# Second block's input products: ten pairs of output tiles by seven block products, and rope keys split in the Fourier phase

## What is computed

```python
# second block
proj = h @ w_in[i]
(s5_u, fq, fk, fv, ff, rw, sq, sk, sv, gates) = _split(proj, IN_SPLIT_SIZES)
y_s5 = _s5_mixer(s5_u, ...)      # bu = einsum(ug, bb); associative_scan; y = einsum(x, c) + d * ug; gelu, glu
...
# first block, in each of its two layers
k_rope = apply_rope(k_r, cos[None], sin[None])
k = concatenate([k_nope, broadcast_to(k_rope, ...)], axis=-1)
```

## Time and profile before

| | us |
|---|---|
| median of three runs | 3330.05 (3327.62 to 3330.68) |
| the profiled execution | 3330.66 |
| its span | 3328.9 |
| PE busy | 3184.9 (96% of the span) |
| DVE busy | 2051.6 (62%) |
| ACT busy | 1010.0 (30%) |
| POOL busy | 937.2 (28%) |

### The profile page before, as it was taken

One profiled execution on the slowest core, in us unless ns is written; L12 is line 12 of the kernel. 1 busy time (PEld: TensorE's weight loads), 2 busy tenths in 40 slices (PEclk: granted clock), 3 DMA queues, 4 the chain that ended last, 5 costly groups with the idle time before them and its releaser, 6 DMA issues. The chain is left out here.

```text
span 3328.9 us, 41783 instructions
## 1 busy us (share of the span) xinstructions
PE 3184.9 (96%) x17082; PEld 2716.1 (82%) x17082; DVE 2051.6 (62%) x2422; ACT 1010.0 (30%) x1456; POOL 937.2 (28%) x617
## 2 busy tenths in 40 slices
PE   8998999999899999999999999999999999999997
PEld 7997888999688898888868986766777787888875
DVE  5535664444476544547466545555676666897788
ACT  2113432101233320000122222555433543444644
POOL 3320001333000033333224322000241453555575
PEclk9999999999999999999999999999999999999998
DMA  3120000211100013323330004111461454455453
GB/s 137 45 65 9 21 1 20 78 45 45 33 29 1 7 45 144 125 104 97 108 129 33 1 29 121 36 45 36 137 221 67 140 166 152 142 178 174 146 158 120
DMA packets 111758, 282.12 MB, mean 85 GB/s; under 512 B 15010, under 2 KB 20770, under 8 KB 111552
## 3 DMA queue, kind: packets, MB, share of 16 engines
q1 hardware_dynamic: 107104, 263.19, 24.2%
q10 hardware_dynamic: 4464, 16.25, 1.2%
HBM read 237.37 MB, written 41.42 MB: 84 GB/s over the span
## 5 line engine op out<-in xcount | busy, mean ns | idle before, releaser
L3672 PE MATMUL psum<-x,w_hi 128*128 128x512 f32 x2016 | 627.0, 392 | 8.3 <-DVE x L3643 3.2
L199 POOL CAST w_hi<-w_raw 128x1024 fp32r<-128x1024 f32 x116 | 125.7, 1083 | 1765.6 <-PE psum L212 1092.5
L3672 PEld LDWEIGHTS psum<-x,w_hi 128*128 128x128 f32 x2016 | 379.0, 189 | 93.5 <-issue 7.0
L3672 PE MATMUL psum<-x,w_lo 128*128 128x512 f32 x1008 | 393.4, 390 | 0.0
L3557 POOL TENSOR_TENSOR w_lo<-w_sum,w_hi 128x512 fp32r<-128x512 f32 x180 | 251.1, 1402 | 333.0 <-ACT w_hi L3551 333.0
L745 PE MATMUL psum<-h,w_hi 128*128 128x512 f32 x1024 | 327.6, 401 | 11.1 <-PEq L126 7.4
L203 POOL TENSOR_TENSOR w_lo<-w_raw,w_hi 128x1024 fp32r<-128x1024 f32 x116 | 302.1, 2605 | 16.4 <-DVE y L1554 7.2
L745 PEld LDWEIGHTS psum<-h,w_hi 128*128 128x128 f32 x1024 | 189.9, 191 | 58.7 <-issue 17.4
L3672 PEld LDWEIGHTS psum<-x,w_lo 128*128 128x128 f32 x1008 | 189.9, 188 | 39.7
L212 PE MATMUL psum<-hn_hi,w_hi 128*128 128x348 f32 x864 | 188.7, 327 | 16.4 <-DVE hn_lo L409 14.9
L745 PE MATMUL psum<-h,w_lo 128*128 128x512 f32 x512 | 202.5, 395 | 0.0
(11 more groups left out here) (464 smaller groups left out, 6468.2 us busy)
## 6 DMA issues: line engine op xcount, KB each, us to landing
w_raw<-in_w_mlp SPq DMA_DIRECT2D x169, 256.0 KB, 2.9
norm_factor<-in_w_mlp SPq DMA_DIRECT2D x87, 256.0 KB, 2.9
w_raw<-in_w_mlp SPq DMA_DIRECT2D x42, 512.0 KB, 3.4
w_raw<-in_w_in SPq DMA_DIRECT2D x36, 512.0 KB, 3.4
w_raw<-in_w_gates SPq DMA_DIRECT2D x32, 512.0 KB, 4.0
gates_kept<-gate_stage SPq DMA_DIRECT2D x64, 256.0 KB, 2.2
gates<-gates_kept SPq DMA_DIRECT2D x32, 512.0 KB, 3.3
w_raw<-in_w_out SPq DMA_DIRECT2D x24, 512.0 KB, 3.5
```

The costliest lines, as they stand in the source:

```text
L199: self.core.nc.gpsimd.tensor_copy(self.hi[:, g % 2], self.raw[:, g % 2]).then_inc(self.hi_done, 1)
L3672: last = self.core.nc.tensor.matmul(out, one[:, k, :], other[:, k, :], start=(group == 0 and k == 0 and part == 0), stop=(group == second ...
```

## The change

The 23 tiles are made in another order and another way. Three tiles stay plain: the two of S5 and the forget gates. The other twenty form ten pairs of neighbours. A pair is a product of a weight of 2x2 blocks (two output tiles by two halves of K) with a right side of 2x2 blocks (two halves of K by two halves of the tokens); it is made by the Strassen-Winograd scheme in seven block products of 4 k-blocks x 3 passes = 12 matmuls of 128x512 (tensor_pair). Each product has its own PSUM bank, eight in turn.

The right-hand sums are made once and kept in SBUF (vector_sums): for kk = 0 to 3 four sums of 128x512, their high parts on ACT (scalar_sums) and their low parts on DVE, from rows of h that ACT has first multiplied in place by the norm weight (scalar_rows). For each pair DVE makes four weight sums (vector_weights, and vector_last_weight for the block S4), ACT the seven high parts, POOL the seven low parts, in a ring of four half-tiles. ACT copies the first product out; DVE adds the others up in four quarters and scales each by r (vector_first, vector_second: seven adds, four scalings), and SP stores each quarter. The rows of h now need only r (one operation of 1024 columns in the first eight pairs).

The S5 parameters move with it: angle after pair 2, coefficients after pair 4, powers after pair 5, shift powers after 6 and 7, fin in the middle of the last pair, and hout goes to the S5 phase (vector_outs), where DVE makes it after all stores have landed. u and ug lie where the sums lay, so SP loads them in the S5 phase too, after the last store and the last product. PE there transposes with ident, no longer with masks, and waits for the rows only after the transposes, and for hout before the Toeplitz row.

In the first block kr_hi and kr_lo are made at the end of the rope step in the Fourier phase; the head tensors are placed below the Fourier ones for that.

```diff
...
+class PairedProducts:
+    A11, A12, S2, S1, S3, S4, A22 = range(7)
+    BANKS = (2, 5, 3, 4, 0, 1, 6, 7)
+    U, X, V, W = range(4)
+    STEPS = 11
+    FREED_BY = (0, 1, 2, 6, 5, 8, 10)
...
+    def store(self, sp, p, i, step):
+        m = PAIRS2[p][0 if i in (self.X, self.V) else 1]
+        cols = slice(0, CH2) if i in (self.X, self.U) else slice(CH2, T2)
+        sp.wait_ge(self.step, self.STEPS * p + step)
+        sp.dma_start(self.io["proj2"][m][:, cols], self.quarter(p, i)).then_inc(self.stored[(4 * p + i) % 6], 16)
...
+    def scalar_rows(self, act, x_lo):
+        for n in range(KT):
+            k = n // 2 + n % 2 * (KT // 2)
+            act.wait_ge(x_lo, k + 1)
+            self.core.nc.scalar.activation(self.rows(k), self.rows(k), ACT.Copy, scale=self.scale(k)) \
+                .then_inc(self.scaled, 1)
...
+    def scalar_weight(self, act, x):
+        p, j = divmod(x, 7)
+        if j in (self.S1, self.S3, self.S2, self.S4):
+            act.wait_ge(self.w_sums, 4 * p + (self.S1, self.S3, self.S2, self.S4).index(j) + 1)
+        else:
+            self.loaded(act, p)
+        if self.before[x] is not None:
+            act.wait_ge(self.done, self.before[x] + 1)
+        self.core.nc.scalar.activation(self.ring(self.w.hi, x), self.source(x), ACT.Copy).then_inc(self.w_hi_done, 1)
...
+    def pool_weight(self, pool, x):
+        pool.wait_ge(self.w_hi_done, x + 1)
+        self.core.nc.gpsimd.tensor_tensor(self.ring(self.w.lo, x), self.source(x),
+                                          self.ring(self.w.hi, x).bitcast(F32), ALU.subtract) \
+            .then_inc(self.w_lo_done, 1)
...
+    def tensor_pair(self, pe, p):
+        nc = self.core.nc
+        for j in range(7):
+            x = 7 * p + j
+            pe.wait_ge(self.w_lo_done, x + 1)
+            if x >= 8:
+                q, freed = divmod(x - 8, 7)
+                if freed == self.A11:
+                    pe.wait_ge(self.copied, q + 1)
+                else:
+                    pe.wait_ge(self.step, self.STEPS * q + self.FREED_BY[freed])
+            dst = self.core.psum[:, self.bank(p, j), :]
+            w_hi, w_lo = self.ring(self.w.hi, x), self.ring(self.w.lo, x)
+            for kk in range(KT // 2):
+                b_hi, b_lo = self.moving(j, kk)
+                if p == 0 and j in (self.S1, self.S3, self.S2, self.A22):
+                    pe.wait_ge(self.t_lo_done, 4 * kk + (self.S1, self.S3, self.S2, self.A22).index(j) + 1)
+                for part, (one, other) in enumerate(((w_hi, b_hi), (w_hi, b_lo), (w_lo, b_hi))):
+                    last = nc.tensor.matmul(dst, one[:, kk, :], other, start=(kk == 0 and part == 0),
+                                            stop=(kk == KT // 2 - 1 and part == 2))
+            last.then_inc(self.done, 1)
...
+    def vector_sums(self, dve, kk):
+        nc, raw = self.core.nc, self.t_raw
+        first, second = slice(0, CH2), slice(CH2, T2)
+        upper, lower = self.rows(kk), self.rows(KT // 2 + kk)
+        dve.wait_ge(self.scaled, 2 * kk + 2)
+        nc.vector.tensor_tensor(raw[:, 0, kk, :], upper[:, second], upper[:, first], ALU.subtract).then_inc(self.t_sums, 1)
+        nc.vector.tensor_tensor(raw[:, 1, kk, :], lower[:, second], upper[:, second], ALU.subtract) \
+            .then_inc(self.t_sums, 1)
+        dve.wait_ge(self.t_sums, 4 * kk + 1)
...
+    def vector_last_weight(self, dve, p):
+        raw, half = self.raw(p), KT // 2
+        dve.wait_ge(self.w_lo_done, 7 * p + self.A12 + 1)
+        dve.wait_ge(self.w_sums, 4 * p + 3)
+        self.core.nc.vector.tensor_tensor(raw[:, 0, half:], raw[:, 0, half:], self.temps[:, 1], ALU.subtract) \
+            .then_inc(self.w_sums, 1)
...
+    def vector_first(self, dve, p):
+        before = self.STEPS * p
+        dve.wait_ge(self.copied, p + 1)
+        self.quarter_free(dve, p, self.X)
+        self.vector_add(dve, p, self.A12, self.X, self.U)
+        self.vector_last_weight(dve, p)
+        self.vector_add(dve, p, self.S2, self.U, self.U)
+        dve.wait_ge(self.step, before + 1)
+        self.vector_scale(dve, p, self.X)
+        dve.wait_ge(self.step, before + 2)
+        self.quarter_free(dve, p, self.V)
+        self.vector_add(dve, p, self.S1, self.V, self.U)
...
+            for p in range(pairs.n):
+                pairs.store(sp, p, pairs.X, 3)
+                sp.wait_ge(pairs.w_lo_done, 7 * (p + 1))
+                if p + 2 < pairs.n:
+                    pairs.load(sp, p + 2)
+                if p == pairs.n - 1:
+                    w.load(sp, g0 + plain)
+                    w.load(sp, g0 + plain + 1)
+                if p < KT:
+                    sp.wait_ge(h_normed, p + 1)
+                    sp.dma_start(io["h_kept"][p], row(p)).then_inc(h_stored, 16)
+                pairs.store(sp, p, pairs.W, 7)
+                pairs.store(sp, p, pairs.V, 9)
+                pairs.store(sp, p, pairs.U, 11)
...
+            for p in range(pairs.n):
+                if p == 0:
+                    x.wait_read_out(pe, plain - 2)
+                    x.wait_read_out(pe, plain - 1)
+                pairs.tensor_pair(pe, p)
...
+            pairs.scalar_rows(act, x.x_lo)
+            store(0)
+            pairs.scalar_sums(act, 0)
+            pairs.scalar_sums(act, 1)
+            store(1)
+            act.wait_ge(w.tile_done, g0 + 2)
+            pairs.scalar_weight(act, 0)
+            pairs.scalar_weight(act, 1)
+            pairs.scalar_sums(act, 2)
+            pairs.scalar_sums(act, 3)
+            act.wait_ge(w.tile_done, g0 + 3)
+            pairs.scalar_weight(act, 2)
+            pairs.scalar_weight(act, 3)
+            store(2)
...
+            tile(0)
+            pairs.vector_sums(dve, 0)
+            pairs.vector_sums(dve, 1)
+            tile(1)
+            pairs.vector_weights(dve, 0)
+            pairs.vector_sums(dve, 2)
+            pairs.vector_sums(dve, 3)
+            tile(2)
+            for p in range(pairs.n):
+                pairs.vector_first(dve, p)
+                if p + 1 < pairs.n:
+                    pairs.vector_weights(dve, p + 1)
                 else:
-                    x.vector_tile(dve, m, stage[:, m % 2, :], ATT_SCALE if query else 1.0)
-                if m < KT:
-                    nc.vector.scalar_tensor_tensor(out=h_all[:, m, :], in0=h_all[:, m, :], scalar=vecs[:, m:m + 1],
-                                                   in1=r, op0=ALU.mult, op1=ALU.mult).then_inc(h_normed, 1)
-                if m == KT + 1:
+                    dve.wait_ge(pairs.w_lo_done, 7 * p + pairs.S1 + 1)
+                    s5.vector_in(dve, 0)
+                    s5.vector_in(dve, 1)
...
+                pairs.vector_second(dve, p)
+                if p < KT:
+                    nc.vector.tensor_tensor(row(p), row(p), r[:, META:META + T2], ALU.mult).then_inc(h_normed, 1)
+                if p == 2:
                     s5.vector_angle(dve)
-                if m == KT + 3:
+                if p == 4:
                     s5.vector_coefficients(dve)
-                if m == KT + 4:
+                if p == 5:
                     s5.vector_powers(dve)
-                if m == KT + 5:
-                    s5.vector_shift_powers(dve)
-                if m in (KT + 6, KT + 7):
-                    s5.vector_out(dve, 0, SC, m - KT - 6)
-                if m in (KT + 8, KT + 9):
-                    s5.vector_out(dve, SC, SC + 1, m - KT - 8)
-                if m in (KT + 10, KT + 11):
-                    s5.vector_in(dve, m - KT - 10)
-    return BranchesEnded(core.weights, x.g0 + N_PROJ2, stored, h_stored)
+                if p in (6, 7):
+                    s5.vector_shift_powers(dve, range(1, 4) if p == 6 else range(4, 7))
...
+            act.wait_ge(kr_ready, 1)
+            for half in range(2):
+                nc.scalar.activation(kr_hi[64 * half:64 * half + 64], slots[0:64, KR, :], ACT.Copy) \
+                    .then_inc(kr_hi_done, 1)
...
+            nc.vector.tensor_tensor(kr, kr, krs, ALU.add).then_inc(kr_ready, 1)
+            dve.wait_ge(kr_ready, 1)
+            dve.wait_ge(kr_hi_done, 2)
+            nc.vector.tensor_tensor(kr_lo[0:64], kr, kr_hi[0:64].bitcast(F32), ALU.subtract)
+            nc.vector.tensor_tensor(kr_lo[64:P], kr_hi[64:P].bitcast(F32), kr_hi[64:P].bitcast(F32), ALU.subtract)
...
-            for half in range(2):
-                nc.scalar.activation(kr_hi[64 * half:64 * half + 64], kr, ACT.Copy).then_inc(kr_hi_done, 1)
...
-            dve.wait_ge(kr_hi_done, 2)
-            nc.vector.tensor_tensor(kr_lo[0:64], kr, kr_hi[0:64].bitcast(F32), ALU.subtract).then_inc(kr_lo_done, 1)
-            nc.vector.tensor_tensor(kr_lo[64:P], kr_hi[64:P].bitcast(F32), kr_hi[64:P].bitcast(F32), ALU.subtract) \
-                .then_inc(kr_lo_done, 1)
...
+    def vector_outs(self, dve):
+        self.link(self.core.nc.vector.memset(self.hout[:], 0.0))
+        for n0, n1 in ((0, SC), (SC, SC + 1)):
+            for part in range(2):
```

(10 more changed lines are left out.)

337 lines of the change are left out of this document (243 added, 94 removed).

## The result

The changed kernel takes **3339.73 us** (median of six runs, 3333.36 to 3347.93) against 3330.36 for the kernel before (six runs): a ratio of 1.0028, with a 95% interval of 1.0016 to 1.0040. It is slower by 9 us. The forecast was 3325.0 with a range up to 3338, so the result lies 1.7 us above the range and on the side that had the smallest chance.

A forecast was written before the change was run, and what follows sets the result against it. PE was taken to bound the input products of the second block. The terms -27.2 + 15.1 + 1.6 + 3 + 12.7 - 10.4 gave -5.2 us against the median of 3330.05, so 3325.0 us, range 3312 to 3338 (8 in 10).

The forecast's parts named there:

- (a): Input products of the second block: 840 matmuls instead of 960, 120 fewer at 0.227 us each, -27.2 us.
- (b): Start of the changed stage: PE waits for DVE's work before the first pair, +15.1 us, then low clock, +1.6.
- (c): Inside the pairs: S5 jobs make DVE late for S4's weight and PE stalls, +3 us (0 to 8).
- (d): End of the stage: row loads and DVE's output coefficients delay PE's return to gate tiles, +12.7 us (9 to 16).
- (e): Head phases: the rope split removes PE's wait for kn_lo and its low clock, -10.4 us in two layers.
- the rule for the clock: After a long idle PE's clock falls: +1.6 us at the stage's start; 1.8 us saved with the head phase's removed wait.
- The prediction's own signs of being wrong: DVE idle before the first pair, stage not about 265 us, or head phases not 5 us earlier each.
- Rival 2: In the pairs DVE becomes the bound, blocked by POOL's subtractions: 3344 us, at half of it 3334; 12%.
- Rival 4: Head phases: rope split gives only the wait itself, PE standing at the next semaphore; +8 against the sum, 3333 us; 6%.
- Rivals 1 and 3: 1: PE stays the bound, start and end covered, 3292.5 us, 2%. 3: the ends cost less, 3314 us, 10%.
- The band: Whole kernel: forecast 3325 with its own band of 3318 to 3332 us, given 70%.

The follow-up runs named there:

- outs_early: Changed kernel; u and ug loads and DVE's output coefficients wait for the last product, not the last stores, and POOL clears hout; 3333.19 us, ratio 1.0013.
- rope_alone: Kernel before with only the rope keys split in the Fourier phase; 3322.41 us against 3328.69, ratio 0.9978.
- jobs_late: Changed kernel; S5 coefficients halved after pairs 4 and 5, powers after 6, shift powers half after 7, half in the S5 phase; 3335.86 us, ratio 1.0021.
- start_waits: Changed kernel; PE waits for the third plain tile's read-out only ahead of product S3, not ahead of the first pair; 3333.14 us, ratio 1.0013.
- start_more: start_all, with first-pair high parts of S3, S4, A22 before ACT's store wait and DVE's sum S4 before the third tile's read-out; 3324.69 us, ratio 0.9993.
- pairs_alone: Changed kernel with the rope split undone, kr_hi and kr_lo made in the head phase again; 3349.91 us, ratio 1.0063.
- rows_early: Changed kernel; SP issues the u and ug loads after the last product without waiting for the last pairs' stores; 3337.47 us, ratio 1.0034.
- start_all: start_waits, with ACT's row scaling and high parts at the start of the stage in another order; 3326.90 us, ratio 0.9996.
- two_tiles: outs_early, with a second gate tile on PE between the transposes and the product with ug, one tile less beside the shifts; 3328.86 us, ratio 1.0002.
- all_mended: Changed kernel with the edits of start_more, jobs_late and two_tiles, and half of fin in the last pair's first half; 3310.38 us, ratio 0.9945.
- all_mended2: all_mended, with weight sum S4 before each pair's first add and the gate weight loads before the last pair's first quarter store; 3308.26 us, ratio 0.9930.

## Why the prediction was wrong, point by point

Each term of its sum, and what the profiled execution has for it:

| term | forecast | measured |
|---|---|---|
| (a) 120 matmuls fewer | -27.2 | -27.2 |
| (b) start: wait, low clock | +15.1, +1.6 | +16.4, +2.5 |
| (c) inside the pairs | +3 | +3.5 of waits, +1.7 of low clock, +1.2 beside |
| (d) end of the stage | +12.7 | +18.9 |
| (e) rope split | -10.4 | -6.8 |
| behind the stage | 0 | -3.6 |
| sum | -5.2 | +6.6 |

(a) and the mechanism of every other term were right: where PE waits, for whom, and in which order. Four sizes were off, and all four to the same side. The step that failed most is the sum for the end of the stage, forecast at +12.7 us and measured at +18.9; the next is the rule for the clock, which kept all that the rope split saved and put nothing behind the new waits in (c) and (d).

The prediction's own signs of being wrong say the same. The stage from the first read-out of before to the gate tiles was to last about 265 us; with S as the common instant it lasts 276.3. From the start of the first pair to E it is 199.2 us where 190 to 198 were forecast, and the wait for the output coefficients, 5.16 us, is not a short one.

**(d) is the largest, 6.2 us.** The last quarter was scaled at E+9.1, not E+7.7: fin took 11.5 us with POOL's split across it, not 10.3. DVE began the coefficients at E+12.4 and not E+10, since stores and their waits took longer. The coefficients took 21.2 us with the memset, against 18.5 to 21.1. So PE could go on at E+33.6, not E+29.5. The last 2.1 us are low clock: 9.2 us for the Toeplitz step, where the prediction took 7.1 from a row at full clock, though it had itself put a wait of about 10 us ahead of the product with ug and a short one right in front of this step. outs_early, where the wait is short, has 7.1 again (1512.15 to 1519.24).

**(e), 3.6 us.** The step at the wait was right (5.2 a layer). What moved into the Fourier phase cost nothing there: the head phase starts at 269.27, before at 269.16. What failed is the sentence that kept all of the gain: the low clock behind a removed wait was booked as saved, but in the profiled execution it came back behind the next wait, 1.7 us in each layer. The trace of rope_alone shows that with nothing else changed, and its median, -7.3 us, agrees. How often it comes back is known from counts only (18 of 24 passes with the split, 1 of 4 without, last section). By them the mean is 0.8 us a layer, an estimate from 1/2 x 1.6, and part of the 3.6 us is then the luck of this pair of executions.

**(c), 3.4 us.** The waits were forecast to half a microsecond, in pairs 5 to 8 behind the S5 jobs, and jobs_late shows that cause. Left out was the low clock behind the first of them: behind 2.03 us of waiting PE took 4.5 us for twelve matmuls instead of 2.7 (1394.98 to 1399.43 in the timeline). Behind the waits of 0.69 and 0.82 us the clock stayed at 1.00. Of the other 1.2 us, 0.7 lie right at the waits: across that of 0.69 us the starts of two matmuls are 1.08 us apart, and the next ones 0.34, where 0.227 is the pitch.

**(b), 2.2 us.** The chain on DVE was right to 1.3 us. The idle 4.4 us behind ACT's eight rows were 4.21:

```profile
1255.88 2.50 DVE L780 TENSOR_TENSOR t_lo<-t_raw,t_hi 128x512 fp32r<-128x512 f32 x4 [4.21 <-ACT t_hi L714]
...
1279.92 1.21 DVE L460 TENSOR_TENSOR stage<-psum,norm_factor 128x1024 f32<-128x1024 f32 x1
```

The sentence "It is DVE work that no longer fits beside 32 us of plain tiles" was true of DVE and not of PE, whose first two products need none of it. By the prediction's own terms the chain without any waiting ends at about 1281.5 and not at 1280 (and a pair's work on DVE adds up to 11.0 us, not 10.7); neither slip changes a term of the sum. That PE waited at all for this chain changed no number of the forecast either, but start_waits and start_more show that most of this term was the place of a wait.

Behind the stage 3.6 us came back that I had not forecast. Between 2430 and 2480 us PE had a clock of 0.97 before and 1.00 after, and two waits of 0.80 and 0.33 us for a gated product are missing. This may be a shift of low-clock stretches, as in (e). It need not come from the change: start_waits has the same code as the changed kernel behind R and took 1800.2 us there, more than the kernel before.

**Rivals.** Rival 2, DVE as the bound of the pairs, gave a fair number (3334 to 3344) for the wrong reason: with the jobs moved only 4 us of the stage go. Rival 4 had the right part (rope), but its size (+8) is more than twice the 3.6 measured, and its mechanism, PE standing at the next semaphore, did not occur. Rivals 1 and 3 had cheaper ends, and both ends cost more. No rival said that a new wait might carry its own low clock and a removed one not give it back; for that (c), (d) and (e) were off by 1.7, 2.1 and up to 3.6 us, together up to 7.4, where the forecast was 5.2 us from no change.

The band was also too narrow for a reason that a single trace can't show. Six runs of the changed kernel spread over 14.6 us, and their mean clock moves with them: 0.983 at a span of 3331.6, 0.979 at 3346.1.

## What to carry to other kernels

Saving work on the bound engine pays only if nothing ahead and behind grows: here 27 us of matmuls were saved and 44 us of waits and low clock put in, most of it at the two seams. When a stage is rewritten, look at each wait of the bound engine and ask which product needs it, put independent work (here a gate tile) into the seam, and follow SP's queue in order, since a load can stand behind a store that waits for something else. And price a new wait of 2 us or more at its length and, for the upper bound, a slow stretch behind it (1.7 us here, behind a wait of 2.03 us in half of the executions); a removed wait is sure only of its length.

## What the runs showed of the hardware

Stretches that no kernel here changes take one of a few times. From the 1.88 us wait in a head phase to the one nearly 180 us later PE needs 178.2 to 178.4 us or 179.7 to 180.0, and nothing between, in all 28 passes of 14 profiled executions (two layers each). In all 28 the long value goes with a mean clock of about 0.91 in the 20 us behind the first wait, and the short one with 1.00. With the rope split the long one came in 18 of 24 passes, without it in one of four, which is few. From the second of these waits to the next layer it is 401.0, 402.3 or 404.0 to 404.3. So one fall of the clock costs some 1.3 to 1.8 us here, and the same code has more or fewer of them in different executions: the 5.8 us of pairs_alone ahead of S are 1.5 up to the first head phase, 1.5 and 3.3 in these two stretches of the first layer, and -0.6 between. The Trainium skill, TensorE: Matmul & The Clock Gate, Part 1, says that the number of slow matmuls at a kernel's start differs between runs of the same kernel; these traces agree (178.2 or 179.9 us for the same code), and show it far from the kernel's start too.

Not every wait brings a fall. The wait for S4 behind the S5 coefficients is 2.03 to 2.05 us long in eight executions; in four of them the clock fell behind it (changed, pairs_alone, rows_early, outs_early), in four it did not (start_waits, start_all, start_more, two_tiles). The 5 us behind it, in the changed kernel and in start_more:

```profile
1394.98:1399.98 5.00, 5.00 (x15) 3.96 (x16) 4.91 (x5) 0.29 (x1) 5.00 (x3) 0.66 0.51 185
```

```profile
1385.64:1390.64 5.00, 5.00 (x22) 4.16 (x23) 4.91 (x5) 0.63 (x1) 5.00 (x3) 1.00 0.54 156
```

Behind the waits of 3.08 to 3.11 us at the start of start_all, start_more, all_mended and all_mended2 it stayed at 1.00 as well. What decides whether a fall comes was not tested.

POOL and DVE hold each other up in both directions. In the changed kernel a sum that takes 0.68 us elsewhere takes 1.75 beside POOL's subtractions, and these 1.67 each instead of 1.30:

```profile
1266.83 1.75 DVE L769 TENSOR_TENSOR t_raw<-h 128x512 f32<-128x512 f32 x1
...
1266.37 3.34 POOL L735 TENSOR_TENSOR w_lo<-pair_w,w_hi 128x512 fp32r<-128x512 f32 x2 [19.59 <-ACT w_hi L725]
```

A memset of 128x4608 took 3.90 us on DVE (changed kernel) and 3.94 on POOL (all_mended), so moving it did not make it longer.
